# TensorE's loop over the expert blocks: six blocks to a turn where there were three

## The chip, the cores and the metric

One NeuronCore of one Trainium2 chip runs the whole kernel. The metric is the device time of one execution in microseconds (us), the median over runs. A profiled execution has a time of its own and a span, from its first to its last instruction. In what follows TensorE (PE) multiplies, VectorE (DVE), ScalarE (ACT) and GpSimd (POOL) do the rest, and SyncE (SP) issues most DMAs.

## The reference, cut to what matters

The reference is one layer: retention and differential attention over a shared input projection, an output projection, a routed mixture of experts, a gate on a per-layer embedding, and a last norm. The change lies in the mixture of experts. Its tokens (512 of width 1024) go each to 2 of 16 experts:

```python
lg = (t @ w_rg) + b_rg                       # 4 groups, top-1
le = (t @ w_re) + b_re                       # 16 experts, top-2 within the group
combine = one_hot(group) * weights_in_group  # (512, 16), two entries a row
...
for gi in range(N_GROUPS):
    sl = slice(gi * EXPERTS_PER_GROUP, (gi + 1) * EXPERTS_PER_GROUP)
    hid = jax.nn.silu(jnp.einsum('td,edf->etf', t, w_gate[sl])) * jnp.einsum('td,edf->etf', t, w_up[sl])
    hid = hid * combine[:, sl].T[:, :, None]
    out = out + jnp.einsum('etf,efd->td', hid, w_down[sl])
```

Everything is float32. An expert has 2 MB each of w_gate, w_up and w_down.

## The kernel before, in words

Each engine has a program of its own; semaphores join them. Up to the experts the programs are straight code: on TensorE the projections, the heads and the output projection, then the router and the first half of the embedding branch.

The experts come next. The 1024 pairs of token and expert are sorted by expert and cut into blocks of at most 64 rows, each block with one expert; their number, `total`, and each block's expert are known only when the kernel runs. With these inputs it is 23, block 0 and blocks 1 to 22; the program allows for up to 31. Expert weights lie in a ring of three slots (`ring_gu`, `ring_dn`), which SP reloads as soon as TensorE is through with the expert that held a slot (lines 602 to 611, with the loads at L569 and L572). POOL gathers a block's rows (`rows`) and scatters its result (`y_blk` to `y_rows`).

For each block `b` TensorE does four things, in `step`: `hidden_transpose(b - 1)` (2 transposes, L1551), `gate_up(b)` (L1539), `rows_transpose(b + 1)` (4 transposes, L1527) and `down(b - 1)` (L1563). Which slot of the ring holds the block's weights is a number read at run time (L1513 and L1514). [...] With the reads of registers, waits and branches a block's code is 337 entries, of which some 140 are run and the rest jumped over.

`over_blocks` (L147 to L161) makes the loop: `Fori` runs a fixed number of turns, and in a turn the body stands `group` times, each copy inside an `If` (L158) that tests whether the block exists; where one doesn't, the rest of the turn is jumped over. The last entries of a turn (L155) count and jump back. VectorE, ScalarE and GpSimd have a loop of the same form with six blocks to a turn, TensorE one with three: 10 turns of 3. After the loop come `hidden_transpose(total - 1)` and `down(total - 1)`.

Then the gate of the embedding branch: SP waits until TensorE is through with the block before expert 14's (L609) and loads `ple_gate_raw` (4 MB) over slot 1; ScalarE and VectorE split it in two (`ple_hi` L879, `ple_lo` L1220); VectorE's copy of the last block's result (`y_blk`, L1200) stands between the sixth and the seventh `ple_lo`. The last scatter, the gathers of all results (`yg`, L625), the sum (`xr`, L1234 and L1235) and TensorE's last matmuls, some 400, follow.

Of the kernel before, what the change touches and what calls it, by code (L numbers as in the profile page):

```python
# [52 lines left out]
MAX_BLOCKS = (TOP_K * SEQ - N_EXPERTS) // BLK + N_EXPERTS  # L53
ROW_BUFS = 3
GROUP = 6
PE_GROUP = 3
TABLE = MAX_BLOCKS + ROW_BUFS
HALF = D // 2
N_PAIRS = TOP_K * SEQ
# [88 lines left out]
MIX_ROWS = [4, 5, 6, 7, 0, 1, 2, 3]  # L148

def over_blocks(engine, total, step, ahead=0, group=GROUP):

    with engine.Fori(0, (MAX_BLOCKS - 1) // group) as turn:  # L155
        def guarded(k):
            b = group * turn + (1 + k)
            with engine.If(b + ahead < total):  # L158
                step(b, k, turn)
                if k + 1 < group:  # L160
                    guarded(k + 1)  # L161

        guarded(0)
# [37 lines left out]
def trunk(nc, x, p, norm_mix, w_in, lam_q1, lam_k1, lam_q2, lam_k2, diff_subln, w_out, norm_ffn,  # L201
# [3 lines left out]
    with ctx:  # L205
# [429 lines left out]
        def _(pool):  # L635
# [42 lines left out]
            def step(b, k, turn):  # L678
# [3 lines left out]
                scatter(b - 1, k % 2, 2 * b + (ROW_BUFS + 1))  # L682

            over_blocks(pool, total, step)
            scatter(total - 1, 2, 2 * total + ROW_BUFS)

        @block.scalar
        def _(act):
# [175 lines left out]
            def step(b, k, turn):  # L865
# [3 lines left out]
                rowsT_evac(b + 1)  # L869

            over_blocks(act, total, step)

# [46 lines left out]
        def _(dve):  # L920
# [287 lines left out]
            def step(b, k, turn):  # L1208
                hiddenT(b + 1)
                hidden(b + 2)  # L1210
                evacuate_y(b + 1, k % 2)

            over_blocks(dve, total, step, ahead=2)

            def split_gate(pieces):
# [66 lines left out]
        def _(pe):  # L1282
# [125 lines left out]
            for step, n, *j in schedule():  # L1408
                if step == "out":
                    unit_part(n, *j)  # L1410
                elif step == "scores" and n < HEADS:
                    scores(n, *j)
                elif step == "scores":
                    ret_scores(n - HEADS, n_mix)
                    n_ret += 1
                elif step == "weights":
                    probs_transpose(n)
                elif step == "product":
                    head_product(n)
                elif step == "mixT":  # L1420
                    mix_transpose(n, n_ret)
                    n_mix += 1
                elif step == "opening":
                    opening(n)
# [84 lines left out]
            total = pe.value_load(cum_i[0:1, N_EXPERTS - 1:N_EXPERTS], min_val=N_EXPERTS, max_val=MAX_BLOCKS)  # L1509
# [13 lines left out]
            def rows_transpose(b, buf, loads):  # L1523

                pe.wait_ge(s_rows[buf], 16 * loads)
                for j in range(4):
                    last = T.transpose(b_xT[:, j * P:(j + 1) * P], rows[buf][:, j * P:(j + 1) * P], ident)  # L1527
                last.then_inc(xT_done, 1)

            def gate_up(b):  # L1530

                def products(s, loads):
                    pe.wait_ge(xT_ready, b + 1)
                    for k in range(KD):
                        if k % (KD // 2) == 0:

                            pe.wait_ge(s_gu[s][k // (KD // 2)], 32 * loads)
                        for q in range(2):
                            last = T.matmul(b_gu[q * BLK:(q + 1) * BLK, :], rowsT[:, k % 4, k // 4, :],  # L1539
                                            ring_gu[s][:, k, :, q * UC:(q + 1) * UC],  # L1540
                                            start=(k == 0), stop=(k == KD - 1))
                        if k == KD // 2 - 1:
                            last.then_inc(gu_half_done, 1)
                    last.then_inc(gu_done, 1)

                in_slot(b, products)

            def hidden_transpose(b):
                pe.wait_ge(hid_ready, b + 1)
                for j in range(2):  # L1550
                    last = T.transpose(b_hT[:, j * P:(j + 1) * P], hid[:, j * P:(j + 1) * P], ident)  # L1551
                last.then_inc(hT_done, 1)

            def down(b):

                def products(s, loads):
                    pe.wait_ge(hidT_ready, b + 1)
                    pe.wait_ge(y_ready, b + 1)
                    pe.wait_ge(s_dn[s], 16 * loads)

                    for kf in range(D_EXPERT // P):
                        for q in range(2):
                            last = T.matmul(b_dn[q * BLK:(q + 1) * BLK, :], hidT[:, kf % 2, kf // 2, :],  # L1563
                                            ring_dn[s][:, kf, q * (D // 2):(q + 1) * (D // 2)],
                                            start=(kf == 0), stop=(kf == D_EXPERT // P - 1))
                    last.then_inc(dn_done, 1)

                in_slot(b, products)
# [7 lines left out]
            def step(b, k, turn):  # L1576
                hidden_transpose(b - 1)
                gate_up(b)
                rows_transpose(b + 1, (2 + k) % ROW_BUFS, PE_GROUP // ROW_BUFS * turn + ((2 + k) // ROW_BUFS + 1))
                down(b - 1)  # L1580

            over_blocks(pe, total, step, group=PE_GROUP)
            hidden_transpose(total - 1)
            down(total - 1)

# [50 lines left out]
```

## Time and profile before

| | us |
|---|---|
| median of 3 runs | 666.97 |
| the three runs | 666.94, 666.97, 673.25 |
| the profiled execution, its time | 673.25 |
| its span | 671.4 |
| busy in it: TensorE matmul / weight load | 611.9 / 385.3 |
| busy in it: VectorE / ScalarE / GpSimd | 215.8 / 202.2 / 59.8 |
| TensorE's clock, mean granted | 0.967 of full speed |

The profiled execution is the slowest of the three by 6.3 us; 1.9 us of its time lie outside the span. A profile tells for every engine when each instruction ran, and what ended the idle time before it. "issue" as the end of an idle time says that the engine waited for nothing that the profile shows. [...]

### The profile page before, as it was taken

The page shows a single profiled execution, that of the slowest core. Times are in us where ns is not written, and L with a number is a line of the kernel's source. Part 1 is how long each engine was busy: PE and PEld are TensorE (multiplying, and loading weights), DVE is VectorE, ACT ScalarE, POOL GpSimd, SP SyncE. Part 2 cuts the span into 40 slices and gives each one's busy share as a digit, 9 for nine tenths or more (in the row PEclk, how much of TensorE's full clock was granted, in tenths as well). Part 3 has the DMA queues.
Part 4 walks back from the last instruction along what each step waited for, and adds up shares of the span by engine and source line. Part 5 has one row for each costly group of instructions (what it writes and reads, how often), then busy time and mean ns, then how long its engine had stood idle before and what let it go on. Part 6 is the DMA issues. An engine that isn't in the chain of part 4 may idle for free.

```text
span 671.4 us, 9274 instructions
## 1 busy us (share of the span) xinstructions
PE 611.9 (91%) x3330; PEld 385.3 (57%) x3331; DVE 215.8 (32%) x480; ACT 202.2 (30%) x440; POOL 59.8 (9%) x105
## 2 busy tenths in 40 slices
PE   2899999999999999996889999999999999925995
PEld 2798877878989899953323333333333333304884
DVE  3612264556254442364011010111111110163563
ACT  5532354545444533332000000101010100152674
POOL 0000000000000000002011212121212212110000
PEclk9999999999999999978989999999999999975998
DMA  8743213112211079763999899997998999935001
GB/s 305 186 171 114 74 64 125 63 55 72 64 63 63 1 280 394 298 256 113 362 329 396 329 386 395 361 358 282 397 399 320 392 395 397 408 121 218 33 32 62
DMA packets 76272, 153.34 MB, mean 228 GB/s; under 512 B 7944, under 2 KB 27024, under 8 KB 75984
## 3 DMA queue, kind: packets, MB, share of 16 engines
q1 hardware_dynamic: 72000, 139.24, 56.9%
q0 software_dynamic: 3952, 12.85, 5.1%
q10 hardware_dynamic: 288, 0.81, 0.3%
q8 instruction: 22, 0.36, 0.2%
q14 instruction: 10, 0.08, 0.0%
HBM read 142.66 MB, written 10.23 MB: 228 GB/s over the span
## 4 chain that ended last, share of the span: by engine, by line
PE 80%; DMA 9%; DVE 3%; ACT 3%; issue 2%; SPq 2%; POOLq 0%; ACTq 0%; DVEq 0%; POOL 0%
PE bank L1539 20%; PE bank L1288 12%; PE bank L1289 12%; PE bank L1290 12%; PE bank L1563 10%; DMA ple_gate_raw<-in_w_ple_gate 4%; PE bank L1365 2%; DMA ring_gu<-in_w_up 2%; PE bank L1486 2%; PE bank L1527 2%; SPq L569 2%; PE bank L1338 2%; DMA small<-const_small 1%; PE bank L1379 1%; PE bank L1551 1%
## 5 line engine op out<-in xcount | busy, mean ns | idle before, releaser
L1539 PE MATMUL bank<-ring_gu,rowsT 128*64 128x512 f32 x736 | 166.6, 605 | 5.1 <-issue 4.1
L1539 PEld LDWEIGHTS bank<-ring_gu,rowsT 128*64 128x64 f32 x736 | 51.4, 139 | 104.2 <-issue 103.1
L1563 PE MATMUL bank<-ring_dn,hidT 128*64 128x512 f32 x368 | 84.0, 598 | 1.4 <-DVE hidT L1191 1.4
L857 ACT ACTIVATE silu_g<-bank 128x256 f32<-128x256 f32 x23 | 8.8, 383 | 240.2 <-PE bank L1539 240.2
L1036 DVE TENSOR_TENSOR w_lo<-w_raw,w_hi 128x2048 fp32r<-128x2048 f32 x18 | 41.3, 2293 | 80.3 <-ACT w_hi L722 71.1
L1186 DVE TENSOR_TENSOR hid<-silu_g,bank 128x256 f32<-128x256 f32 x23 | 9.7, 422 | 169.7 <-ACT silu_g L857 169.7
L1288 PE MATMUL bank<-w_hi,hT_hi 128*128 128x256 f32 x192 | 55.9, 291 | 0.0
L1289 PE MATMUL bank<-w_lo,hT_hi 128*128 128x256 f32 x192 | 54.9, 286 | 0.0
L1290 PE MATMUL bank<-w_hi,hT_lo 128*128 128x256 f32 x192 | 54.8, 286 | 0.0
L1288 PE MATMUL bank<-hT_hi,w_hi 128*128 128x512 f32 x128 | 50.8, 397 | 0.0
L1563 PEld LDWEIGHTS bank<-ring_dn,hidT 128*64 128x64 f32 x368 | 24.4, 136 | 44.7 <-issue 44.7
L1289 PE MATMUL bank<-hT_lo,w_hi 128*128 128x512 f32 x128 | 49.9, 390 | 0.0
L1290 PE MATMUL bank<-hT_hi,w_lo 128*128 128x512 f32 x128 | 49.9, 390 | 0.0
L1200 DVE COPY y_blk<-bank 128x512 f32<-128x512 f32 x23 | 15.9, 692 | 74.2 <-PE bank L1563 74.2
L1288 PEld LDWEIGHTS bank<-w_hi,hT_hi 128*128 128x128 f32 x192 | 37.5, 195 | 1.1 <-issue 1.1
L1289 PEld LDWEIGHTS bank<-w_lo,hT_hi 128*128 128x128 f32 x192 | 37.5, 195 | 0.0
L1290 PEld LDWEIGHTS bank<-w_hi,hT_lo 128*128 128x128 f32 x192 | 37.4, 195 | 0.0
L722 ACT ACTIVATE w_hi<-w_raw 128x2048 fp32r<-128x2048 f32 x18 | 34.3, 1906 | 0.0
L649 POOL COPY src_now<-src_row 128x1 int32 (+1 forms) x26 | 5.2, 199 | 315.7 <-DVE dst_row L1014 307.7
L1288 PE MATMUL bank<-ple_hi,x2T_hi 128*128 128x512 f32 x64 | 26.5, 414 | 2.5 <-issue 2.5
L1288 PEld LDWEIGHTS bank<-hT_hi,w_hi 128*128 128x128 f32 x128 | 24.0, 188 | 8.0 <-issue 3.3
L657 POOL DMA_INDIRECT rows<-h_rows,src_now x26 | 25.7, 989 | 20.7 <-POOL src_now L649 20.7
(208 smaller groups left out, 898.0 us busy)
## 6 DMA issues: line engine op xcount, KB each, us to landing
ring_gu<-in_w_gate SPq DMA_DIRECT2D x32, 1024.0 KB, 13.6
ring_gu<-in_w_up SPq DMA_DIRECT2D x32, 1024.0 KB, 15.1
ring_dn<-in_w_down SPq DMA_DIRECT2D x16, 2048.0 KB, 12.3
w_raw<-in_w_in SPq DMA_DIRECT2D x14, 1024.0 KB, 5.0
w_raw<-in_w_out SPq DMA_DIRECT2D x4, 1024.0 KB, 5.0
ple_gate_raw<-in_w_ple_gate SPq DMA_DIRECT2D x1, 4096.0 KB, 26.0
yg<-y_rows SPq DMA_DIRECT2D x8, 512.0 KB, 7.0
xr<-in_x SPq DMA_DIRECT2D x4, 512.0 KB, 7.5
```

The lines of the kernel that those rows point to most:

```text
L569: sp.dma_start(ring_gu[slot][:, ks, n, :], src[:, ks, :]).then_inc(s_gu[slot][half], 16)
L657: pool.indirect_dma_start(out=rows[buf][:], out_offset=None, in_=h2_rows, in_offset=rows_of).then_inc(s_rows[buf], 16)
L722: nc.scalar.activation(w_hi[u % 2][:], w_raw[u % 2][:], ACT.Copy).then_inc(hi_done, 1)
L1036: V.tensor_tensor(w_lo[u % 2][:], w_raw[u % 2][:], w_hi[u % 2][:].bitcast(F32), ALU.subtract).then_inc(lo_done, 1)
L1200: V.tensor_copy(y_blk[buf][:], b_dn[:]).then_inc(y_ready, 1)
L1288: T.matmul(o, w_of(w[0], k), m_of(m[0], k), start=(k == 0), stop=False)
L1289: T.matmul(o, w_of(w[0], k), m_of(m[1], k), start=False, stop=False)
L1290: last = T.matmul(o, w_of(w[1], k), m_of(m[0], k), start=False, stop=(k == KD - 1))
L1338: last = T.matmul(b_score[2 * (i % 2) + c][:, 0:L], dqT[64 * c:64 * c + 64, h, i * P:(i + 1) * P], dkT[64 * c:64 * c + 64, h, 0:L], start= ...
L1365: last = T.matmul(b_o[:, i * P:(i + 1) * P], probsT[n % 2][:, o:o + P], v[:, j, h * P:(h + 1) * P], start=(j == 0), stop=(j == i))
L1539: last = T.matmul(b_gu[q * BLK:(q + 1) * BLK, :], rowsT[:, k % 4, k // 4, :], ring_gu[s][:, k, :, q * UC:(q + 1) * UC], start=(k == 0), st ...
L1563: last = T.matmul(b_dn[q * BLK:(q + 1) * BLK, :], hidT[:, kf % 2, kf // 2, :], ring_dn[s][:, kf, q * (D // 2):(q + 1) * (D // 2)], start=( ...
```

## The change

`over_blocks` loses its argument `group`, and TensorE's loop has six blocks to a turn like those of the other engines: 5 turns of 6. The number of loads to wait for, which `rows_transpose` is given, is computed for the new turn. Nothing else is touched: the same instructions are run on the same data in the same order, apart from the jumps at the turns' ends.

```diff
-PE_GROUP = 3
...
-def over_blocks(engine, total, step, ahead=0, group=GROUP):
+def over_blocks(engine, total, step, ahead=0):
...
-    with engine.Fori(0, (MAX_BLOCKS - 1) // group) as turn:
+    with engine.Fori(0, (MAX_BLOCKS - 1) // GROUP) as turn:
         def guarded(k):
-            b = group * turn + (1 + k)
+            b = GROUP * turn + (1 + k)
             with engine.If(b + ahead < total):
                 step(b, k, turn)
-                if k + 1 < group:
+                if k + 1 < GROUP:
                     guarded(k + 1)
...
-                rows_transpose(b + 1, (2 + k) % ROW_BUFS, PE_GROUP // ROW_BUFS * turn + ((2 + k) // ROW_BUFS + 1))
+                rows_transpose(b + 1, (2 + k) % ROW_BUFS, GROUP // ROW_BUFS * turn + ((2 + k) // ROW_BUFS + 1))
                 down(b - 1)

-            over_blocks(pe, total, step, group=PE_GROUP)
+            over_blocks(pe, total, step)
```

In the built program of TensorE the loop grows from 1,014 entries to 2,023, and the whole program from 5,651 to 6,660. Before, the third block's products by `down` end the turn (each row is one of the three copies; the `ISA` and `REGISTER_ALU` rows are register work; L155 counts and jumps back, and what follows is the code behind the loop):

```order
L1559 REGISTER_ALU
L1563 MATMUL bank<-ring_dn_162,hidT 64x512 x8
L1520 UNCONDITIONAL_BRANCH
L155 REGISTER_ALU
L155 COMPARE_AND_BRANCH
L1551 MATMUL bank<-small,hid 128x128 x2
```

With the change the same place of TensorE's program, the end of the third block, goes on to a fourth (the line numbers are lower by one):

```order
L1558 REGISTER_ALU
L1562 MATMUL bank<-ring_dn_162,hidT 64x512 x8
L1519 UNCONDITIONAL_BRANCH
L157 REGISTER_ALU
L157 COMPARE_AND_BRANCH
L1550 MATMUL bank<-small,hid 128x128 x2
```

The jump back has moved behind the sixth block, 2,021 entries from the loop's start where it was 1,012; in its place stands the test whether the next block exists.

## Rows read from the trace of the kernel before

**Rows 1.** The page: busy time and the queues; packets, MB, share of 16 engines.

```profile
PE 611.9 (91%) x3330; PEld 385.3 (57%) x3331; DVE 215.8 (32%) x480; ACT 202.2 (30%) x440; POOL 59.8 (9%) x105
q8 instruction: 22, 0.36, 0.2%
```

**Rows 2.** TensorE in order of time, the fourth block of the loop: start, us, what.

```profile
362.97 3.65 PE L1563 MATMUL bank<-ring_dn,hidT 128*64 128x512 f32 x16
366.56 0.44 PE L1551 MATMUL bank<-small,hid 128*128 128x128 f32 x2
366.92 7.09 PE L1539 MATMUL bank<-ring_gu,rowsT 128*64 128x512 f32 x32
```

**Rows 3.** The chain that ended last, behind the blocks: start, us, what.

```profile
564.70 26.04 DMA ple_gate_raw<-in_w_ple_gate
...
592.10 4.06 DVE ple_lo L1220 x6
596.16 0.61 DVE y_blk L1200
```

**Rows 4.** Instruction fetches (q8) from 326 to 402 us; packets, MB, share.

```profile
q8 instruction: 4, 0.07, 0.3%
```

**Rows 5.** All DMA queues in one answer, from 402 to 624 us.

```profile
q1 hardware_dynamic: 26210, 66.01, 79.0%
```

**Rows 6.** TensorE's sequencer, jumps back (L155): count, ns min/median/max, first and last start.

```profile
L155 PEldq COMPARE_BRANCH  x10: 86/211/219, 363.1 to 585.0; - x10
```

**Rows 7.** Straight code between two fetches: PE and PEld counts, clock, DMA, GB/s.

```profile
145.86:164.10 18.24, 18.24 (x126) 15.69 (x125) 9.56 (x29) 9.14 (x29) 0.00 (x0) 1.00 0.36 116
```

**Rows 8.** The sequencer's jumps that took longer than their like, and one of the like.

```profile
L1515 PEldq COMPARE_BRANCH  x1: 342/342/342, 320.5 to 320.5; - x1
...
L1515 PEldq COMPARE_BRANCH  x1: 301/301/301, 335.7 to 335.7; - x1
...
L1518 PEldq COMPARE_BRANCH  x1: 3713/3713/3713, 338.1 to 338.1; - x1
...
L1515 PEldq COMPARE_BRANCH  x1: 349/349/349, 353.4 to 353.4; - x1
...
L1518 PEldq COMPARE_BRANCH  x1: 294/294/294, 397.7 to 397.7; - x1
...
L1518 PEldq COMPARE_BRANCH  x1: 169/169/169, 467.0 to 467.0; - x1
```

**Rows 9.** Instruction fetches in 0.2 us from 324.1, 339.3, 357.1 and 401.3.

```profile
q8 instruction: 1, 0.02, 27.9%
...
q8 instruction: 1, 0.02, 33.9%
...
q8 instruction: 1, 0.02, 34.0%
...
q8 instruction: 1, 0.02, 34.6%
```

**Rows 10.** TensorE in order of time, the second block of the loop.

```profile
339.22 0.44 PE L1551 MATMUL bank<-small,hid 128*128 128x128 f32 x2
342.11 8.78 PE L1539 MATMUL bank<-ring_gu,rowsT 128*64 128x512 f32 x32 [2.45 <-issue]
```

**Rows 11.** TensorE by stretch: us, busy (x), granted clock, DMA share, GB/s.

```profile
342.11:350.89 8.78, 8.78 (x33) 0.81 1.02 391
355.36:362.45 7.09, 7.09 (x34) 1.00 1.04 399
593.00:609.20 16.20, 0.00 (x0) 0.59 0.46 172
609.20:613.00 3.80, 1.97 (x8) 0.50 1.01 413
```

**Rows 12.** The sequencer at the loop's end: tests that fail, and the last branch.

```profile
L158 PEldq COMPARE_BRANCH  x2: 214/216/218, 583.1 to 583.9; - x2
...
L1515 PEldq COMPARE_BRANCH  x1: 80/80/80, 586.7 to 586.7; - x1
```

**Rows 13.** The sequencer's branch to the products of the loop's fourth block.

```profile
L1515 PEldq COMPARE_BRANCH  x1: 90/90/90, 365.1 to 365.1; - x1
```

**Rows 14.** TensorE in order of time, the last block behind the loop.

```profile
588.39 3.65 PE L1563 MATMUL bank<-ring_dn,hidT 128*64 128x512 f32 x16 [1.39 <-DVE hidT L1191]
```

**Rows 15.** TensorE in order of time, the second half of a `gate_up`.

```profile
555.69 3.65 PE L1539 MATMUL bank<-ring_gu,rowsT 128*64 128x512 f32 x16 [0.15 <-DMA ring_gu<-in_w_up]
```

## The prediction

> **What bounds the kernel now.** I read the page first: TensorE is busy for 91% of the span [rows 1]. In order of time the expert blocks follow each other without a gap: from one `gate_up` to the next it is 7.09 us of `gate_up`, the transposes, 3.65 us of `down`, and the next `gate_up` starts as the transposes end [rows 2]; that is 11.56 us a block, at full clock [rows 11]. So in blocks 3 to 22 TensorE is the bound, and what its sequencer does is hidden as long as the queue isn't empty. Behind the blocks the chain leaves TensorE: the load of `ple_gate_raw` starts when block 19 is through and takes 26.04 us, then six `ple_lo`, then VectorE's copy of the last block's result at 596.16 [rows 3]. TensorE's last product ended at 592.04 (588.39 + 3.65) [rows 14], so the last block has 4.1 us of cover; what delays block 19 or one before it has none.
>
> The change touches only jumps, so the next views are the sequencer's and the instruction fetches'. Jumping back costs 211 ns, nine times (the tenth branch falls through) [rows 6], and none of it shows on TensorE. There is nothing to gain from jumping back less often.
>
> **How the program arrives.** TensorE's program comes in 22 pieces of 16 KB (0.36 MB) [rows 1]. Between two of them, in straight code, stand 251 matmuls and weight loads and a few waits [rows 7]; so a piece is 256 entries of 64 bytes, and 22 borders in a program of 5,651 entries are one fetch for each: nothing is fetched twice. In the loop of before that is seen directly: four fetches up to 402 us [rows 4], the last at 401.3, and from there to 624 us the answer has the data queues and no q8 row [rows 5]. The loop's 1,014 entries stay at the engine for all turns.
>
> Where the borders lie follows from the slow jumps. Four jumps took 342, 301, 349 and 294 ns where their like take 169, and after each of them a fetch starts 3.7 us later (320.5 and 324.2, 335.7 and 339.4, 353.4 and 357.2, 397.7 and 401.4) [rows 8, 9]: a jump into a new piece asks for the next. In entries from the loop's start they go from -142 to -9, 268 to 339, 690 to 758 and 977 to 1,012, and the stalled one of 3,713 ns from 421 to 489. Borders 23 to 39 entries ahead of the loop and every 256 from there fit all (the second of them was crossed in sequence just ahead of its jump, which was the first to ask). The stalled jump tells the price: its piece was asked for at 335.7 and could be used at 338.1 + 3.7 = 341.9, **6.2 us** later.
>
> **The change, part by part.** The loop of before reaches into 5 pieces, with the one behind it 6 are held. The new loop's last entries are 2,021 and 2,022; the ninth piece begins between 2,009 and 2,025. So in one turn 9 or 10 pieces pass through the engine. The trace of before shows that 6 stay, and nothing above: whether 9 stay is the unknown. Its bounds are the two rows: no fetch at all in a later turn [rows 5], and a fetch and a wait at every jump into a dropped piece [rows 8]. I take the second, since the only count that is shown to be held is well under nine, and work it out:
>
> First turn: blocks 1 to 3 as now. Blocks 4 to 6 are new code, where before it was held; each piece is asked for one piece ahead, 8.8 us of work (256 of a block's 337 entries, of 11.56 us) against 6.2 us. I take 0; the bound is one stall like the one seen, 2.45 us idle and 1.7 us at the lower clock (8.78 against 7.09 us) [rows 10, 11], 4.1 us.
>
> Jumps back after blocks 6, 12 and 18: the loop's first piece has been dropped for the last ones. The sequencer waits 6.2 us. What hides it is TensorE's queue: at the jump of 363.1 TensorE had `down` ahead, and the next `gate_up` was ready to issue at 365.4 (the branch of 365.1 and two register steps) for a start at 366.92 [rows 13, 2]: 1.5 us of cover. That leaves 4.7 us idle; after the 2.45 us the clock fell to 0.5 for a while and `gate_up` took 1.7 us more [rows 10, 11], so I add 1.7: 6.4 us each, **19.2 us**, all ahead of block 19's end and so on the path.
>
> The loop's end: before, the test after block 22 fails at 583.1, two more turns of nothing follow, and the sequencer is out by 585.1 [rows 12, 6]. Now the failing test in the fourth turn jumps to the end piece (dropped when the first piece came back), from there back to the first (dropped again), the fifth turn's test jumps to the end piece once more: three waits, 3 x 6.0 us more than the short jumps, less 0.8 us for the one turn fewer. So out at 602.4 on the old scale. `down(22)` needs another 1.8 us (the branch at 586.7 and the start at 588.39 are the second half of such a step) [rows 12, 14]: start at 604.2 instead of 588.39, 15.8 us late. TensorE has then done nothing but two transposes since 586.6, over 15 us, and after such an idle time its clock is 0.50 [rows 11], so 3.65 us become up to 7.3. End at 611.5 against 592.04, 19.5 us late, less the cover of 4.1: **15.3 us**. The load of `ple_gate_raw` is over by then.
>
> Sum: 0 + 19.2 + 15.3 = 34.5 us. The profiled execution would go from 673.25 to 707.8; it lay 6.3 us over the other two, and against the median of 666.97 the same sum gives **701.5 us**.
>
> The other engines have their six blocks as before. SP's reloads wait for TensorE, so they start later by as much; TensorE waited 0.15 us for one of them [rows 15], which a later TensorE waits no more. POOL, ScalarE and VectorE only follow.
>
> [...]
>
> **The rivals.** (a) *All pieces stay.* For it: the new loop is 2,023 entries and before shows no limit. Against: it is twice what was shown to be held. Then only blocks 4 to 6 of the first turn are cold: 0 to 4.1 us, and the time is 667 to 671, no measurable change. This is the case on the other side, and it decides by one thing, whether nine pieces are held. (b) *Only the jumps back miss.* If the ninth piece begins behind entry 2,021 (4 of 17 places), the end piece is the eighth and is held; one wait is left at the end, hidden but for a microsecond: 19 to 20 us, 686. (c) *A miss is cheaper.* If a demanded piece takes only the 3.7 us that the stalled jump itself took, the jumps back leave 2.2 us idle without a lower clock, 6.6 us, and the end some 4 to 8: 678 to 682. (d) *Every piece is dropped in turn.* If the oldest piece goes each time, the later turns refetch all: as in the first turn, one stall of 4.1 us in 5 pieces, 24 pieces in three turns, up to 20 us more, while the end has one or two waits instead of three, 3 to 9 us less its cover: 700 to 715. It would look like my forecast in time and unlike it in place. (e) *Faster*: the sequencer's work of 0.6 us a turn would have to be on the path; before shows no gap there [rows 2]. Four turns fewer would be 2.4 us, under what counts.
>
> **How the numbers follow.** Forecast and (d), which meet in 696 to 712: 0.52. (b), 682 to 692: 0.14. (c), 676 to 684: 0.13. (a), 666 to 672: 0.15. Above 712: 0.04, faster or anything else: 0.02. The range leaves out (a) and the tail above: 676 to 713. A measurement of this kernel can tell about 1% from no change, which is 660.3 to 673.6: faster 0.02, same 0.15, slower 0.83.
>
> **What would show it.** The page's q8 row: 22 + 4 = 26 for the longer program alone; with the first two pieces and the last two fetched again in every turn, 34 to 44; with (d) 48 or more. L154's jumps back with a largest value near 6,200 ns (3,700 by (c), 219 by (a)). TensorE idle for "issue" ahead of the transposes or the products of blocks 7, 13 and 19, 4 to 5 us each, and a long idle ahead of the last `down`. I am wrong if q8 has some 26 packets and the jumps back take 211 ns.

## The result, and the profile after

| | before | changed |
|---|---|---|
| median, us | 666.97 | 701.29 |
| the runs, us | 666.49, 666.94, 666.97, 667.01, 673.25 | 699.50, 700.80, 701.29, 704.85, 705.22 |
| ratio, 95% interval | | 1.0509 [1.0459, 1.0560] |
| span of the profile shown, us | 671.4 | 701.0 |
| q8 fetches of 16 KB | 22 | 55 |

The changed kernel is 5.1% slower. Busy times of VectorE, ScalarE and GpSimd are the same within 0.1 us; TensorE's is 5.8 us longer for the same 3,330 matmuls, at a mean granted clock of 0.949 instead of 0.967. Against [rows 1], the page of the changed kernel:

```profile
PE 617.7 (88%) x3330; PEld 384.7 (55%) x3331; DVE 215.9 (31%) x480; ACT 202.1 (29%) x440; POOL 59.9 (9%) x105
...
q8 instruction: 55, 0.90, 0.5%
```

The program has 6,660 entries and so 26 borders of 256; the other 29 fetches brought a piece that had been there before. From 397 to 472 us, the second turn, the DMA view has eight fetches, where the kernel before had none from 402 us to the end of its loop [rows 5]:

```profile
q8 instruction: 8, 0.13, 0.8%
```

The sequencer's jumps back (L154 now) against [rows 6], and the tests of L157; the columns are count, ns min/median/max, first and last start:

```profile
L154 PEldq COMPARE_BRANCH  x5: 86/6151/6762, 393.1 to 617.3; - x5
...
L157 PEldq COMPARE_BRANCH  x24: 73/83/3590, 319.2 to 616.7; - x24
...
L154 PEldq COMPARE_BRANCH  x1: 4029/4029/4029, 612.5 to 612.5; - x1
...
L154 PEldq ALU_OP  x1: 36/36/36, 609.6 to 609.6; - x1
```

Where one took 211 ns, the first three take 6.15, 6.76 and 6.15 us; the fourth, after the last block, 4.03 us; and the test that jumps over the absent blocks 3.59 us. Between these two lies a third wait: the entry that counts (`ALU_OP`, last row) ran at 609.6, and the jump behind it, 0.1 us later in the kernel before, started at 612.5. The jump is the loop's last entry and the only one in its ninth piece (e1 below). TensorE in order of time at the first jump back, to be held against [rows 2]:

```profile
384.89 7.09 PE L1538 MATMUL bank<-ring_gu,rowsT 128*64 128x512 f32 x32
391.91 0.66 PE L1526 MATMUL bank<-small,rows 128*128 128x128 f32 x4
392.50 3.65 PE L1562 MATMUL bank<-ring_dn,hidT 128*64 128x512 f32 x16
399.59 0.43 PE L1550 MATMUL bank<-small,hid 128*128 128x128 f32 x2 [3.44 <-issue]
402.32 9.35 PE L1538 MATMUL bank<-ring_gu,rowsT 128*64 128x512 f32 x32 [2.30 <-issue]
```

The jump starts at 393.1, 0.6 us after `down` began, and ends at 399.2. `down` runs on meanwhile, all of it, to 396.15: what was handed to TensorE before the jump, its queue, is worked off without the sequencer (by that name go the trace's PEldq rows of branches and register work). Then TensorE waits twice for it: 3.44 us for the fetch, and 2.30 us more: the sequencer's register reads and branches ahead of `gate_up` end at 402.3, where `gate_up` starts. With work in the queue they are hidden: behind the jump of 363.1 in the kernel before, `gate_up` has no idle time ahead of it [rows 2]. The windows show the idle time and the clock behind it (us, busy, granted clock, DMA share, GB/s):

```profile
384.89:391.98 7.09, 7.09 (x34) 1.00 1.05 398
402.32:411.67 9.35, 9.35 (x33) 0.75 1.02 382
619.34:625.97 6.63, 6.63 (x16) 0.54 0.01 2
```

The waits of TensorE, whole kernel (us in total, times, longest):

```profile
PE bank L1550 <- issue: 19.6, 4, 8.0
...
PE bank L1538 <- issue: 11.5, 6, 2.4
```

**Where the 29.6 us between the two spans are.** A block takes 11.56 us when nothing waits. From the `gate_up` ahead of a jump back to the next one it is 17.43, 17.52 and 17.84 us, so 5.87, 5.96 and 6.28 us more, and the three `gate_up` behind the jumps take 9.35, 9.81 and 9.88 us instead of 7.09. That makes 8.1, 8.7 and 9.1, together 25.9 us. One more wait of 2.40 us stands ahead of `gate_up` of block 20:

```profile
556.05 0.43 PE L1550 MATMUL bank<-small,hid 128*128 128x128 f32 x2 [4.37 <-issue]
558.26 9.88 PE L1538 MATMUL bank<-ring_gu,rowsT 128*64 128x512 f32 x32 [1.78 <-issue]
...
575.09 7.09 PE L1538 MATMUL bank<-ring_gu,rowsT 128*64 128x512 f32 x32 [2.40 <-issue]
```

The end, by the chain that ended last (start, us, what), against [rows 3] and [rows 14]:

```profile
609.46 7.99 issue
617.45 0.69 PE bank L1550 x2
...
618.17 0.44 DVE hidT L1190
...
619.34 6.66 PE bank L1562 x16
...
626.02 0.70 DVE y_blk L1199
```

The chain no longer comes from `ple_gate_raw` but from TensorE, and the copy of `y_blk` is at 626.02 instead of 596.16. The last `gate_up` starts at 598.20, 22.8 us later than in the profile of before, so the end itself costs 7.0 us. What is missing in 25.9 + 2.4 + 7.0 = 35.3 lies ahead: at block 6 the changed kernel was 5.2 us *ahead*. Its blocks began 3.3 us sooner, and its stall ahead of block 2's `gate_up` was 1.25 us without a lower clock, where before had 2.45 us and lost another 1.7 [rows 10]; its `gate_up` of block 0 took 1.0 us more (9.70 against 8.74). Not all of this is the change: whatever the kernel, the profiles of this case start block 0 at 312.5 to 312.9, at 314.2 or at 316.2 to 316.7. The profile of before is the slowest of its five runs, 6.3 us above their median. That the other four lack those 5.2 us would bring the 35.3 us together with the medians' 34.3; no profile of one of them was kept, so this is not shown.

### The profile page after: what moved, and what is told of

The parts are those of the page before. It is cut to its first block, busy times and chain, and to the rows that moved or that the text cites. A ratio compares the mean times of both kernels' runs of the same rounds, so it can differ in the third digit from the quotient of the medians.

```text
span 701.0 us, 9250 instructions
## 1 busy us (share of the span) xinstructions
PE 617.7 (88%) x3330; PEld 384.7 (55%) x3331; DVE 215.9 (31%) x480; ACT 202.1 (29%) x440; POOL 59.9 (9%) x105
## 3 DMA queue, kind: packets, MB, share of 16 engines
HBM read 142.66 MB, written 10.23 MB: 218 GB/s over the span
## 4 chain that ended last, share of the span: by engine, by line
PE 85%; issue 6%; DVE 3%; ACT 3%; DMA 3%; POOLq 0%; DVEq 0%; POOL 0%; ACTq 0%; SPq 0%
PE bank L1538 25%; PE bank L1562 12%; PE bank L1287 12%; PE bank L1289 11%; PE bank L1288 11%; PE bank L1364 2%; PE bank L1526 2%; PE bank L1485 2%; PE bank L1337 1%; PE bank L1550 1%; DMA small<-const_small 1%; PE bank L1378 1%; PE bank L1447 1%; ACT w_hi L721 1%; PE bank L1592 1%
## 5 line engine op out<-in xcount | busy, mean ns | idle before, releaser
L1538 PE MATMUL bank<-ring_gu,rowsT 128*64 128x512 f32 x736 | 173.4, 626 | 12.3 <-issue 11.5
L1538 PEld LDWEIGHTS bank<-ring_gu,rowsT 128*64 128x64 f32 x736 | 53.5, 144 | 116.4 <-issue 116.4
L1562 PE MATMUL bank<-ring_dn,hidT 128*64 128x512 f32 x368 | 87.0, 616 | 1.2 <-DVE hidT L1190 1.2
L721 ACT ACTIVATE w_hi<-w_raw 128x2048 fp32r<-128x2048 f32 x18 | 34.3, 1906 | 0.0
L1550 PE MATMUL bank<-small,hid 128*128 128x128 f32 x46 | 10.3, 306 | 20.0 <-issue 19.6
```

Of the source, the lines that this page charges most:

```text
L721: nc.scalar.activation(w_hi[u % 2][:], w_raw[u % 2][:], ACT.Copy).then_inc(hi_done, 1)
```

## The experiments

The rivals: the length of the loop or of the jump back costs as such; six blocks in a turn cost for another reason; the 6.2 us are the fetch's own, or made by the weights' traffic. Each ratio is against the kernel before on the same chip, which took 671.0 us beside e1 to e4, 670.3 beside e5 to e8 and 670.4 beside e9; the changed kernel ran beside 666.97, so that times of different chips compare to a few us only.

**e1: three blocks, a far jump back.** Unused code inside a test that never holds makes the loop as long as in the changed kernel, 2,023 entries:

```diff
                 down(b - 1)
+                if k == PE_GROUP - 1:
+                    with pe.If(total < b):
+                        for j in range(252):
+                            T.matmul(b_gu[0:BLK, :], rowsT[:, j % 4, 0, :], ring_gu[0][:, j % KD, :, 0:UC], start=True, stop=True)
```

> Three blocks to a turn as before, but behind the third block stand 1,008 entries of matmuls inside a test that never holds, so the loop is 2,023 entries long and the jump back as far as in the changed kernel, while only 8 pieces of 16 KB are entered or asked for in a turn. If what counts is how many pieces a turn brings in, and 8 are held: the first jump over the unused code misses once (about 6 us, of which 4 to 5 show), later turns fetch nothing, 668 to 674 us, some 28 fetches. If the length of the loop or of the jump back is what costs: a wait of 6 us at each of seven or more jumps back, 8 us each on the path, 715 to 730 us. If fewer than 8 pieces are held: fetches in every turn and a time in between.

Measured: 696.24 us, ratio 1.0403 [1.0352, 1.0455], 27 fetches. The time is in neither of the two expected ranges, and though it lies between them, the fetches in every turn that were to go with that are absent; the rows decide. The jumps back (L155), and the jumps over the unused code (L1582):

```profile
L155 PEldq COMPARE_BRANCH  x10: 76/208/233, 369.1 to 606.9; - x10
...
L1582 PEldq COMPARE_BRANCH  x7: 214/217/7592, 357.0 to 592.9; - x7
```

Jumping back 2,021 entries takes 208 ns, and from 418 to 610 us, five turns, no piece is fetched. Length and distance cost nothing. The loss is in the first two jumps over the unused code, 6.2 and 7.6 us, each followed by a second wait of 5.6 to 5.9 us before the jump back could start (369.1, where the jump had begun at 357.0). The loop's last two entries lie on both sides of a border: two pieces had to come in a row, and TensorE was idle for 9.0 and 10.6 us. Two things were wrong in what I expected: that double wait, and that the second turn would find these two pieces still there.

**e6: the same with the last two entries in one piece.** 980 unused entries instead of 1,008 (`range(245)`).

> Three blocks to a turn with 980 unused entries behind the third, where there were 1,008: the two last entries of the loop no longer lie on both sides of a piece's border. If the 12 us at the first jump over the unused code were two fetches in a row, one for each side, there is one of 6 us now, at most twice: 672 to 682 us. If the long jump itself costs 12 us: 690 to 700 us as with 1,008.

Measured: 687.40 us, ratio 1.0262 [1.0230, 1.0295].

```profile
L1582 PEldq COMPARE_BRANCH  x7: 214/217/7612, 358.2 to 584.7; - x7
...
365.12 0.43 PE L1551 MATMUL bank<-small,hid 128*128 128x128 f32 x2 [3.24 <-issue]
367.33 10.09 PE L1539 MATMUL bank<-ring_gu,rowsT 128*64 128x512 f32 x32 [1.78 <-issue]
```

The double wait is gone: one of 6.17 us in the first turn, one of 7.61 in the second, none after. The time is 5 us above the range, since I priced a wait at 4 to 5 us of path: the first costs 3.24 + 1.78 idle and 3.0 us of lower clock, 8.0 us, the second 9.5. The three jumps back of the changed kernel cost 8.1, 8.7 and 9.1. So the long jump as such costs nothing; a missing piece does.

**e2, e5, e3: the same six blocks in less code.** `in_slot` writes a block's products three times, once for each slot of the ring, and branches to one of the three copies. With these inputs some of them are never used at some of the six places. They are left out, so what is run and computed is the same but for a test fewer (for e2, one of them):

```diff
-            def in_slot(b, products):
+            def in_slot(b, products, kept=(0, 1, 2)):
...
+                if len(kept) == 2:
+                    with pe.If(slot < kept[1]):
+                        products(kept[0], loads)
+                    with pe.Else():
+                        products(kept[1], loads)
+                    return
...
-                gate_up(b)
+                gate_up(b, KEPT_GU.get(k, (0, 1, 2)))
```

e2 leaves out one copy, the loop has 1,955 entries:

> The changed kernel without one copy of the gate_up products that these inputs never use (slot 0 in the first of the six blocks): loop of 1,955 entries, 8 pieces entered and a ninth asked for. All that is run is the same. If 8 pieces are held and the oldest goes first: still a miss at every jump back, 697 to 702 us, over 45 fetches. If only the ninth entered piece did the harm (9 held): 667 to 672 us, 26 fetches.

e5 leaves out four, three of `gate_up` and one of `down`, 1,783 entries:

> The changed kernel without three unused copies of gate_up's products and one of down's: loop of 1,783 entries, 32 more than in the run without four, and the difference puts its last entries into the eighth piece, which asks for the ninth. If 8 pieces are held and the one asked for ahead counts: misses at jumps back come again, 680 to 700 us and over 35 fetches. If the length of code counts smoothly or the ninth doesn't count: as without four, 666 to 670 us.

e3 leaves out four of `gate_up`, 1,751 entries:

> The changed kernel without four such unused copies: six blocks to a turn, loop of 1,751 entries, 7 pieces entered and an eighth asked for. If 8 pieces are held: jumps back at 0.2 us, 25 fetches, 666 to 671 us, no different from the kernel before. If the six blocks or the longer jump as such cost: near 700 us. If fewer than 8 are held: over 45 fetches and near 700 us.

| | entries | pieces entered + asked for | time, us | ratio, 95% interval | fetches |
|---|---|---|---|---|---|
| changed | 2,023 | 9 + 1 | 701.29 | 1.0509 [1.0459, 1.0560] | 55 |
| e2 | 1,955 | 8 + 1 | 684.75 | 1.0215 [1.0162, 1.0268] | 42 |
| e5 | 1,783 | 8 + 1 | 690.65 | 1.0302 [1.0267, 1.0337] | 45 |
| e3 | 1,751 | 7 + 1 | 668.19 | 0.9979 [0.9952, 1.0007] | 25 |
| before | 1,014 | 5 + 1 | | 1 | 22 |

The jumps back of e2, e5 and e3:

```profile
L156 PEldq COMPARE_BRANCH  x5: 86/6082/6567, 394.5 to 601.5; - x5
...
L156 PEldq COMPARE_BRANCH  x5: 86/7218/7535, 394.1 to 606.7; - x5
...
L156 PEldq COMPARE_BRANCH  x5: 86/211/218, 393.8 to 580.4; - x5
```

Between e5 and e3 lie 32 entries, less than a tenth of a block, and 22.5 us. That is the step at 8 pieces, the one asked for ahead included; six blocks in a turn (e3, 0.9979) cost nothing. In e5 not every jump back misses: the first two took 7.54 and 7.33 us, the third 0.22, the one after the last block 7.22. e2 was forecast near 700 and came out at 685. Its three jumps back between blocks miss as foreseen, but the one after the last block took 0.22 us, and from the last `gate_up` to the copy of `y_blk` pass 16.8 us instead of the changed kernel's 27.8; that is most of the difference. Its fetches differ too: in its third turn, from 477 to 546 us, this is all that the DMA view shows, with no q8 row:

```profile
q1 hardware_dynamic: 8842, 20.70, 81.3%
q0 software_dynamic: 800, 2.62, 9.5%
```

With nine pieces in eight places and the oldest dropped each time, every turn would fetch all nine. The second turn of e2 did, the third didn't: the eight pieces it entered were all there. The next fetch starts at 547.1, and the jump back at 548.1 misses again (6.08 us). So which piece goes is not simply the oldest; e1 and e6 say the same, where eight would have fitted and two were fetched twice.

**e4: one turn fewer.** `Fori` makes 4 turns where there were 5 (23 blocks need no more).

> The changed kernel with 4 turns of TensorE's loop where there are 5 (23 blocks need no more): the wait of the last jump back, 4.0 us, and one test go; the wait of the jump over the absent blocks, 3.6 us, stays. If the end's waits are on the path in full: 4 to 5 us less than the changed kernel, 695 to 698 us. If the copy of y_blk waits for ple_lo anyway: 700 to 702 us.

Measured: 696.66 us, ratio 1.0403 [1.0354, 1.0452], against 701.29 us and 1.0509 of the changed kernel on another chip. The profiles tell it without the chips' difference: `y_blk` is copied at 620.24, 22.3 us after the last `gate_up` starts (597.95), where the changed kernel takes 27.8.

```profile
597.95 7.09 PE L1538 MATMUL bank<-ring_gu,rowsT 128*64 128x512 f32 x32
...
612.85 0.68 PE L1550 MATMUL bank<-small,hid 128*128 128x128 f32 x2 [3.64 <-issue]
615.00 5.19 PE L1562 MATMUL bank<-ring_dn,hidT 128*64 128x512 f32 x16 [1.47 <-DVE hidT L1190]
```

The wait of 4.0 us after the last block is gone, and 5.5 us with it: the end's waits are on the path.

**e7 and e8: reloads of weights made small.** Each reload of an expert brings 8 of 128 partitions, so the products of experts 3 to 15 use mostly older weights; the count of DMAs is the same. e7 is the changed kernel, e8 the one before, with this edit:

```diff
-                sp.dma_start(ring_dn[slot][:],
-                             w_down[bass.ds(e, 1)].rearrange("o (k p) f -> p (o k) f", p=P)).then_inc(s_dn[slot], 16)
+                sp.dma_start(ring_dn[slot][0:rows],
+                             w_down[bass.ds(e, 1)].rearrange("o (k p) f -> p (o k) f", p=P)[0:rows]).then_inc(s_dn[slot], 16)
...
-                load_dn(e, slot)
+                load_dn(e, slot, rows=8)
```

> The changed kernel, but a reload of an expert's weights brings 8 of 128 partitions (the number of DMAs is the same; the products of experts 3 to 15 use mostly the weights of older experts). If a fetch's 6.2 us come from standing behind the weights' traffic: the jumps back wait 3.5 to 4.5 us, and this kernel is 15 to 25 us over its counterpart with three blocks. If the 6.2 us are the fetch's own: jumps back at 6.1 us and 33 to 36 us between the two.

> The kernel before with the same small reloads, the counterpart: TensorE sets the pace anyway and the load of ple_gate_raw is quicker without rivals, 655 to 668 us; 22 fetches, no waits at jumps back.

Measured: 684.96 and 664.16 us, 20.8 us between them where the full kernels have 34.3; 55 and 22 fetches, as with the full loads. The jumps back of e7 and e8:

```profile
L154 PEldq COMPARE_BRANCH  x5: 86/3575/4169, 395.0 to 600.5; - x5
...
L155 PEldq COMPARE_BRANCH  x10: 86/210/219, 356.3 to 577.8; - x10
```

With the same fetches the wait of a jump back falls from 6.2 to 3.6 us. The fetch itself takes 1.1 us in the one and 0.9 in the other; it starts 3.7 us after the first jump back in the changed kernel (396.8 for 393.1) and 1.0 us after it in e7 (396.0 for 395.0). So the weights' traffic makes some 2.6 us of each wait. On the path that is more: the three jumps back cost 9.6 us together in e7, with a lower clock only once, and 25.9 in the changed kernel. The difference between e7 and e8 is still 20.8 us, since in e8 the copy of `y_blk` no longer waits for `ple_lo` (16.8 us after the last `gate_up` instead of 20.8), so that e7's end has no cover and costs 10.5. It fits that the changed kernel's waits behind the last block, with hardly any DMA left (18 GB/s from 605 to 625 us), are 3.6 and 4.0 us.

**e9: the kernel before with its borders moved.** 68 entries ahead of the loop, 64 of them never run, shift the loop against the pieces:

```diff
+            last_block = pe.value_load(cum_i[0:1, N_EXPERTS:], min_val=N_EXPERTS - 1, max_val=MAX_BLOCKS - 1)
+            with pe.If(total < last_block):
+                for j in range(16):
+                    T.matmul(b_gu[0:BLK, :], rowsT[:, j % 4, 0, :], ring_gu[0][:, j % KD, :, 0:UC], start=True, stop=True)
             rows_transpose(0, 0, 1)
```

> The kernel before with 68 entries ahead of the loop, most of them behind a test that never holds, so that the pieces' borders lie 94 entries ahead of the loop and every 256 from there. The blocks of the first turn then enter each new piece by a jump that asks for the next one early. If the idle time ahead of the second block's gate_up is a late fetch: it goes, and 1 to 4 us with it, 663 to 668 us. If it has another reason: it stays, same time.

Measured: 667.24 us against 670.40, ratio 0.9956 [0.9933, 0.9979], a small gain. Ahead of block 2's `gate_up` [rows 10] the wait is gone:

```profile
335.27 0.44 PE L1551 MATMUL bank<-small,hid 128*128 128x128 f32 x2
335.64 7.09 PE L1539 MATMUL bank<-ring_gu,rowsT 128*64 128x512 f32 x32
```

Its ratio is the lowest of the versions that compute the same, though its interval meets that of e3. It holds for this length of program; an edit ahead of the loop moves the borders again.

## Why the prediction was right

**The bound and where a gain could lie.** Right. TensorE's chain has no slack up to block 19, every idle microsecond there is in the time, and fewer jumps back gave nothing: e3 has five turns like the changed kernel and stands at 0.9979 [0.9952, 1.0007].

**How the program arrives, and the borders.** Right, and shown. The 22 fetches of the kernel before and of e9 and the 25 of e3 are each piece once; how many more come in the others (55, 45, 42 and 27) the forecast doesn't give. The border between the loop's entries 2,021 and 2,022 was found by e1's double wait, and e9 moved the borders on purpose. Blocks 4 to 6 in their first turn cost nothing, as taken.

**What is held.** The choice, nine pieces don't stay, was right, and the number is 8: e3, with 7 + 1, jumps back over its seven pieces in 211 ns and takes 668.19 us; e5, with 8 + 1, waits 7.2 to 7.5 us at three jumps back and takes 690.65. The forecast chose between two bounds on one ground, that six held are well under nine; the trace of before gives no number for the limit.

**The jumps back.** The mechanism was right, the size was off: 19.2 forecast, 25.9 us measured. The wait was as taken (6.15 to 6.76 against 6.2). The idle time was taken as 4.7 us and came to 5.7, 5.8 and 6.2. The cover of 1.5 us came from a turn in which the jump began 0.1 us after `down`, with 2.1 us of register work between it and `gate_up`; at the first jump of the changed kernel these were 0.6 and 3.0 us. At the third the jump itself started 1.5 us after the entry that counts (549.6 for 548.0), since it stands alone in the ninth piece: a wait that the forecast didn't have. The lower clock cost 2.3 to 2.8 us each instead of 1.7.

**What happens in the rest of a turn.** The forecast took the rest of a turn as held, with a mark of 34 to 44 fetches; rival (d) said refetches everywhere, and that is how it went: 55 fetches, with (d)'s mark at 48 or more. But they arrive in time, all but one (2.4 us) on the way to block 22. Of the 20 us that (d) allowed for these, little came.

**The end.** Off by a factor of two: 15.3 forecast, 7.0 measured. I took three waits of 6.2 us. There were three, but of 3.6, 2.8 and 4.0 us, and not all in the places named: the price came from rows under full weight traffic (e7 shows what it makes), the wait of 2.8 us stood between the loop's last two entries, and the last test found its piece (0.24 us), which had been fetched just before. The last `down` ran 3.0 us longer at the lower clock, as foreseen; the cover of 4.1 us held.

Sum: 25.9 + 2.4 + 7.0 = 35.3 against 34.5. That the total fits within a microsecond is luck in part: the term for the jumps back was 6.7 us too small, a wait of 2.4 was not in the sum, and the term for the end was 8.3 too large.

**The rivals.** (a), all stays, is out by the fetches. (b)'s condition was met to the letter, since the ninth piece begins behind entry 2,021, but what it drew from that didn't come: the eighth piece was not held at the end, and the jump into it waited 3.6 us. (c), 3.7 us a miss, is wrong under traffic (6.15 to 6.76 us at the jumps back) and right without it (3.3 to 4.2 us, e7); (e) is out by e3.

## What to carry to other kernels

TensorE's loop has a size in instructions, every copy in its body counted, run or not, as far as its pieces are entered or follow one that is. Count 16 KB pieces (256 entries, a float32 product of these blocks being four) with the one asked for ahead, and keep the loop at 8 or fewer: with 7 + 1 this kernel took 0.9979 of the time before (e3), with 8 + 1 1.0302 (e5). Where jumps left some out, even 8 cost two late fetches in the second turn, a wait of 7.6 us (e1, e6). Unrolling pays only for what isn't hidden: here the jumps back, 211 ns each, were hidden and six blocks to a turn bought nothing, while going over the limit, by two pieces, cost three waits of 6 us in 23 blocks, each 8 to 9 us on the path; by one piece (e5, e2) it cost 14 to 20 us. A jump whose duration is in microseconds (6.15 to 6.76 here), together with "issue" ahead of TensorE (19.6 us on L1550) and a higher count in the instruction queue (55 for 22), was the sign; take the price from a stretch with the same DMA traffic, and add the register work that loses its cover and the lower clock.

## What the runs showed of the hardware

- A float32 product of the blocks is two matmuls and two weight loads. `gate_up` writes 16 products a block, and the page of the kernel before counts 736 matmuls and 736 weight loads for its 23 blocks (L1539), 32 and 32 a block; `down` writes 8, and it counts 368 and 368 (L1563), 16 and 16. e1's 252 unused products are 1,008 entries of the built program. A transpose is one of each: 46 and 46 for 46 of them (L1551).
- The queue "q8 instruction" brings TensorE's program: where only that program differed, its packets went from 22 to 55 (27 in e1 and e6, 42, 25, 53 and 45 in e2 to e5) and the other instruction queue, q14, stayed at 10 (11 in e5); and the fetch at 396.8 follows TensorE's jump at 393.1. The reads from HBM that the page counts are 142.66 MB with 22 packets and with 55, so they don't tell where the pieces come from.
- A missing piece took 6.1 to 6.8 us from the jump to use under full weight traffic (DMA share 0.92 over the changed kernel's blocks, 326 to 550 us), 3.3 to 4.2 us when the weights' traffic was away (share 0.30 over e7's blocks, 326 to 545 us) or over (3.6 and 4.0 us in the changed kernel). Where two fetches started within 0.8 us of each other (e1, e5, e6) it was 7.2 to 7.6 us.
- A jump into a piece asked for the next one: behind four jumps of the kernel before a fetch starts 3.7 us later [rows 8, 9]. A border that was passed in sequence didn't at once (in the kernel before the piece behind the loop's end was asked for only at 397.7, by the first jump across the last border, though the border had been passed in the first turn) [rows 8]. By this reading it makes the stall of 2.45 us in the first turn; in e9, built on it, `gate_up` follows the transposes at once (335.64 after 335.27).
- Jumping over 980 or 1,008 entries into a piece that is there takes 214 to 217 ns (e6, e1), no more than the failing tests at the end of the kernel before, 214 to 218 ns [rows 12].
- Which piece is dropped isn't settled: e2's third turn and the second fetches of e1 and e6 don't fit the oldest. No run here was made to tell the rule.
- After 5 to 7 us of idle time the following `gate_up` took 8.6 to 10.1 us instead of 7.09 (changed kernel, e2, e4 to e6). After 2.45 us it took 8.78 (before), after 1.25 and 2.40 us 7.09 (changed kernel), and in e6 8.55 after 1.77 us. So in these runs the clock doesn't fall at one idle time.
